# Three buffers instead of four for rounded weight tiles, and one expert chunk loaded earlier

## The reference

```python
h = rms_norm(x, g_mix)
proj = h @ w_in + b_in                       # q, k, v, r, gates, ...
mixed = sigmoid(gate_a) * (o_a @ w_gla_out) + sigmoid(gate_b) * (o_b @ w_swa_out)
x = x + mixed @ w_out
logits = rms_norm(x, g_ffn) @ w_router + b_router        # top 4 of 32
u = xb @ w_e1[e] + b_e1[e]                   # for each expert: 1024 x 2048
act = clamped_swiglu(u)
y = act @ w_e2[e] + b_e2[e]                  # 1024 x 1024
out = rms_norm(x + combine(y), g_final)
```

## Time and profile before

| what | value |
|---|---|
| median of 3 executions | 1175.7 us (1175.5 to 1176.05) |
| the profiled execution | 1175.9 us, its span 1174.1 us |
| PE busy | 1125.6 us (96%) |
| DVE, ACT, POOL busy | 434.7, 257.0, 38.0 us |
| read from HBM | 446.12 MB |
| mean granted clock of TensorE | 0.998 |

### The profile page before, as it was taken

One profiled execution on the slowest core, in us unless ns is written; L12 is line 12 of the kernel. 1 busy time (PEld: TensorE's weight loads), 2 busy tenths in 40 slices (PEclk: granted clock), 3 DMA queues, 4 the chain that ended last, 5 costly groups with the idle time before them and its releaser, 6 DMA issues.

```text
span 1174.1 us, 17495 instructions
## 1 busy us (share of the span) xinstructions
PE 1125.6 (96%) x7259; PEld 538.5 (46%) x7259; DVE 434.7 (37%) x832; ACT 257.0 (22%) x445; POOL 38.0 (3%) x30
## 2 busy tenths in 40 slices
PE   7999999999999999999999999999999999999997
PEld 6987889983333333333333333333333333333332
DVE  6889956954322222222222222222222222222223
ACT  5467745332111111111111111111111111111112
POOL 1001600011000000000000000000000000000000
PEclk9999999999999999999999999999999999999999
DMA  8645337789999999999999999999999999999995
GB/s 298 231 155 206 144 136 268 283 354 420 427 428 427 435 430 429 430 444 431 438 433 429 436 429 435 438 433 433 431 435 431 424 431 434 432 432 430 431 424 236
DMA packets 23202, 447.66 MB, mean 381 GB/s; under 512 B 2736, under 2 KB 3120, under 8 KB 5344
## 3 DMA queue, kind: packets, MB, share of 16 engines
q1 hardware_dynamic: 22736, 446.76, 90.2%
q10 hardware_dynamic: 432, 0.42, 0.1%
HBM read 446.12 MB, written 1.05 MB: 381 GB/s over the span
## 4 chain that ended last, share of the span: by engine, by line
PE 58%; DMA 29%; DVE 9%; ACT 2%; issue 1%; POOL 1%; DVEq 0%; SPq 0%; another core or an unknown queue 0%; ACTq 0%
PE PS L943 35%; DMA EXT<-wexp 20%; PE PS L667 11%; DMA ring<-wexp 8%; PE PS L936 3%; PE PS L928 3%; PE PS L959 2%; DVE slot_R L1361 1%; PE PS L716 1%; DVE ROW L1817 1%; DVE ROW L1820 1%; DVE BRW L1813 1%; DVE ROW L1814 1%; DVE SM L1549 1%; DVE ring L1544 1%
## 5 line engine op out<-in xcount | busy, mean ns | idle before, releaser
L943 PE MATMUL PS<-ring,MX 128*64 128x512 f32 x1536 | 349.6, 597 | 11.3 <-DMA ring<-wexp 10.7
L943 PEld LDWEIGHTS PS<-ring,MX 128*64 128x64 f32 x1536 | 103.6, 136 | 221.6 <-issue 199.5
L1308 ACT ACTIVATE TAB<-BRW 128x256 f32<-128x256 f32 x64 | 26.7, 417 | 587.0 <-DVE BRW L1813 587.0
L943 PE MATMUL PS<-EXT,MX 128*64 128x512 f32 x512 | 116.9, 598 | 7.9 <-DMA EXT<-wexp 7.8
L943 PE MATMUL PS<-ring,TAB 128*64 128x512 f32 x512 | 120.0, 600 | 4.1 <-DMA ring<-wexp 4.1
L943 PE MATMUL PS<-EXT,TAB 128*64 128x512 f32 x512 | 119.5, 598 | 0.5 <-DMA EXT<-wexp 0.5
L1813 DVE TENSOR_SCALAR BRW<-PS 128x256 f32<-128x256 f32 x64 | 27.2, 425 | 241.2 <-PE PS L943 241.2
L667 PE MATMUL PS<-slot_R 128*128 128x256 f32 (+2 forms) x288 | 90.2, 313 | 0.0
L1361 DVE TENSOR_TENSOR slot_R<-ring,slot_R 128x2048 fp32r<-128x2048 f32 (+1 forms) x37 | 83.1, 2262 | 13.4 <-ACT slot_R L1100 13.1
L1100 ACT ACTIVATE slot_R<-ring 128x2048 fp32r<-128x2048 f32 (+1 forms) x38 | 70.8, 1869 | 45.2 <-PE PS L667 24.1
L936 PE MATMUL PS<-MX,BRW 64*128 64x512 f32 x264 | 74.2, 640 | 0.8 <-DVE MX L1832 0.8
(11 more groups left out here) (263 smaller groups left out, 1083.4 us busy)
## 6 DMA issues: line engine op xcount, KB each, us to landing
ring<-wexp SPq DMA_DIRECT2D x23, 4096.0 KB, 41.4
ring<-wexp SPq DMA_DIRECT2D x22, 2048.0 KB, 13.0
EXT<-wexp SPq DMA_DIRECT2D x10, 4096.0 KB, 40.1
ring<-wblk SPq DMA_DIRECT2D x36, 1024.0 KB, 4.9
EXT<-wexp SPq DMA_DIRECT2D x13, 2048.0 KB, 13.8
ring<-wexp SPq DMA_DIRECT2D x8, 1024.0 KB, 10.4
EXT<-wexp SPq DMA_DIRECT2D x6, 1024.0 KB, 47.6
BRW<-brow SPq DMA_DIRECT2D x7, 256.0 KB, 5.1
```

Of the source, the lines that this page charges most:

```text
L943: last = mm(PS[g * SLOTS:(g + 1) * SLOTS, b, :], lhsT, rhs[:, g * 512:(g + 1) * 512], start=start, stop=stop)
L1308: fn(SGM[h], GLU, ACT.Sigmoid, scale=ALPHA).then_inc(sgm_ready, 1)
```

## The change

- `h_slot`: up to unit 28 (`GIVEN`) the rounded tiles go round four places as before, from unit 29 on round three of them. `split(u)` waits for the unit that held its place, `held_before`; for units 32 to 37 this is `u - 3` instead of `u - 4`.
- The place that is given up is next to slot 0, and the two slots take chunk 4. `C_FIRST` (chunk 4) leaves the list `MIDDLE` and is issued right after the weight load of unit 34 (`FIRST_AT`), that is, once unit 29 has been multiplied. `last_of` gives the unit after which a slot is free.
- ACT rounds the last two parts of the mixed tensor before `split(36)`, not after it.
- DVE's `rest(36)` moves from before the reads of block 16 to after them.

```diff
-W_SLOTS = [1, 2, 4, 6, 8]
-H_SLOTS = [3, 5, 7, 9]
+W_SLOTS = [2, 3, 4, 6, 8]
+H_SLOTS = [1, 5, 7, 9]
...
-MIDDLE.insert(1, C_SQ)
+C_FIRST = MIDDLE.pop(0)
+MIDDLE.insert(0, C_SQ)
...
+GIVEN = 2 * BLOCKS.index("glao1")
+FIRST_AT = GIVEN + 6
...
+        def h_slot(u):
+
+            if u <= GIVEN:
+                return (u - GIVEN) % len(H_SLOTS)
+            return 1 + (u - GIVEN - 1) % (len(H_SLOTS) - 1)
+
+        def held_before(slot_fn, u):
+
+            return max((n for n in range(u) if slot_fn(n) == slot_fn(u)), default=None)
+
+        def last_of(slot_fn, q):
+
+            return max(n for n in range(NU) if slot_fn(n) == q)
...
-            return slot(H_SLOTS[(u - (NU - len(H_SLOTS))) % len(H_SLOTS)], rounded)[:, 0:unit_width(u)]
+            return slot(H_SLOTS[h_slot(u)], rounded)[:, 0:unit_width(u)]
...
-                elif c in MIDDLE:
+                elif c in MIDDLE or c == C_FIRST:
                     for n in (2 * s, 2 * s + 1):
                         if n in W_SLOTS:
-                            multiplied(sp, NU - len(W_SLOTS) + W_SLOTS.index(n))
+                            multiplied(sp, last_of(w_slot, W_SLOTS.index(n)))
                         elif n in H_SLOTS:
-                            multiplied(sp, NU - len(H_SLOTS) + H_SLOTS.index(n))
+                            multiplied(sp, last_of(h_slot, H_SLOTS.index(n)))
...
                 if u == FREE_AT:
                     first_chunk(C_FREE)
+                if u == FIRST_AT:
+                    first_chunk(C_FIRST)
...
                 landed(act, u)
-                if u >= len(H_SLOTS):
-                    multiplied(act, u - len(H_SLOTS))
+                held = held_before(h_slot, u)
+                if held is not None:
+                    multiplied(act, held)
                 fn(h_unit(u, True), w_unit(u), ACT.Copy).then_inc(hi_ready, 1)
...
             split(NU - 3)
-            split(NU - 2)
             for c in range(2, 4):
                 act.wait_ge(mix_ready, c + 1)
                 fn(MIX2[0][:, 2 * c:2 * c + 2, :].rearrange("p k t -> p (k t)"), MIX[c], ACT.Copy).then_inc(mix_hi, 1)
+            split(NU - 2)
             split(NU - 1)
...
                     rest(35)
-                    rest(36)
+            rest(36)
             rest(37)
```

## The result

The changed kernel takes 1178.34 us (median of 14 executions, 1176.32 to 1180.23) against 1176.14 us for the kernel before beside it (14 executions, 1175.38 to 1177.57). The ratio is 1.0018, 95% interval 1.0011 to 1.0025: 2.2 us slower, 0.18%. The forecast was 1175.5 us with a range up to 1177.6 us; the time lies 0.7 us above the range. The profiled execution took 1177.18 us (span 1175.3 us).

The account below looks back on a forecast made before the run. The prediction took DMA throughput as the bound. PE's 2.3 us wait minus 2.0 to 3.1 us of queue removed gave +0.3 to -0.8 us, middle -0.2 us: 1175.5 us against the median 1175.7 us, range 1173.2 to 1177.6 us.

Parts of the forecast that it names:

- The sum: Chunk 2's time moves by PE's 2.3 us wait minus 2.0 to 3.1 us of queue; middle -0.2 us.
- a rival at 0.10: Clock halves in PE's new wait; a half unit, 2.9 us of work, runs slow: 1178.3 us in the middle; chance 0.10.
- the stall: PE's wait in block 15's second half near 220.7 us for a bank whose read stands behind rest(32): 2.3 us, once.
- The row that I had: Behind the last matmul the granted clock is 1.00 for 2.0 us, then 0.68 over 0.6 us, then 0.50.
- the queue removed: Transfers queued in front of chunk 2, issued at 263.83 us, that loading chunk 4 early takes away: 2.0 to 3.1 us.
- by bytes: Queue in front of chunk 2 reckoned from bytes moved between 241.09 and 272.10 us: 2.0 us.
- by landings: Queue in front of chunk 2 from times to landing, 10.3 us against chunk 4's 7.2 us: 3.1 us.
- The thin covers downstream: Later bank reads and roundings stay ahead of PE despite DVE's delay; thinnest at block 16, 1.3 us.
- The collision of chunk 4 with unit 35's load: Unit 35's load, at worst behind chunk 4, lands by about 231 us, hidden with 4 us to spare.
- The end is set by DMA: DMA throughput sets the end: share 1.00 at 432 GB/s from 300 to 1155 us; PE has 23.1 us of slack.
- Parts 3 and 4: The moved roundings on ACT and the moved rest(36) on DVE cost nothing.
- The first rival: PE's new wait is absent or covered, so 2.0 to 3.1 us are gained: 1172.6 to 1173.7 us; chance 0.12.

Follow-up runs that it names:

- buffers_only: Changed kernel with chunk 4 issued where it was before, after unit 33 and ahead of chunk 10: 1179.02 us, ratio 1.0021.
- fill_stall: Changed kernel with 18 matmuls of 128 x 256, whose result nobody reads, added on PE inside its wait for the bank: 1176.67 us, ratio 1.0010.
- half_stall: Changed kernel with DVE's rest(32) cut in two, the second half behind the first two reads of block 14: 1175.32 us, ratio 0.9993.
- no_stall: Changed kernel with DVE's rest(32) moved behind block 14's reads and biases1(1): 1173.97 us, ratio 0.9985.
- before_again: The kernel before, run again with no edit: 1175.72 us, ratio 0.9999.
- before_pause: The kernel before with 12 matmuls of 128 x 256, whose result nobody reads, added in unit 34: 1175.97 us, ratio 0.9996.
- after_again: The changed kernel, run again with no edit: 1178.07 us, ratio 1.0018.

## Why the prediction was wrong

**What failed.** The sum has no term for the clock: it takes 1.00 throughout, and leaves the fall to a rival at 0.10. That step failed. The fall is the commonest case, in 11 of the 14 executions, and it puts 1.4 to 1.5 us on top of the stall. I held against it that PE is busy without a gap on both sides. The runs showed that this does not save it: the clock fell 1.2 us after PE had resumed in one profile and at once in another (buffers_only), and stayed low for about 3.4 us of full work. The row that I had, 2.0 us at full clock behind the last matmul and less after it, spoke for far more than 0.10. The rule that the prediction cited for this rival (the Trainium skill, TensorE: Matmul & The Clock Gate, Part 1) agrees in kind with the profile in which the clock is 0.52. How short a wait is enough, and what the fall costs, only the runs show. The rival's price was off too: 2.9 us for a half unit of work at half clock, where 1.4 to 1.5 us was measured. That its 1178.3 us is near the measured 1178.34 us is luck: the price of the fall is 1.4 us too high, and the rest of the sum 1.2 us too low.

**The queue in the sum was mis-sized as well.** With the stall at full clock I forecast 1175.5 us; fill_stall, which is that case, takes 1176.67 us. The stall was right (2.37 us against 2.3 us). For the queue removed I took the middle between 2.0 us by bytes and 3.1 us by landings, about 2.5 us. The early chunk was worth 2.0 us against the kernel before, and 1.6 us against the kernel that differs in it alone. So the figure by bytes was the nearer one, and averaging the landings in made 0.5 to 0.9 us of the 1.2 us. The rest is not settled. It lies within the spread of single executions: five of fill_stall's 11 take 1177.98 us or more at an unchanged clock, and the other six 1176.09 to 1176.67 us. The first profile of the changed kernel shows the same spread. PE's delay is that of fill_stall's profile to 0.01 us, but from the weight load of unit 33 to the issue of the last long link it has 860.52 us against 859.82 us in fill_stall (859.27 us in the kernel before), so 0.7 us lie between two executions that have the stall and the early chunk in common and no fall of the clock.

How the queue runs dry can be seen between 264 and 268 us, before and after:

```profile
264.00:268.00 4.00, 3.40 (x27) 1.42 (x25) 2.66 (x8) 2.56 (x6) 2.73 (x3) 1.00 1.06 438
```

```profile
264.00:268.00 4.00, 4.00 (x28) 2.73 (x26) 1.29 (x3) 2.56 (x6) 1.66 (x2) 1.00 0.79 295
```

A share of 1.06 becomes 0.79. This is the cap on the gain and not one more cost: fill_stall and half_stall, profiled at 1176.09 and 1175.03 us, have the same dip (0.79 and 0.80, both 279 GB/s). It also fits the bytes. A lone chunk has moved 6.3 us after its issue, and 4.85 us of that is transfer, so its bytes begin some 1.4 us after the issue; chunk 2's then begin at about 267.6 us, while those of chunk 7, which landed at 267.6 us, had ended about 0.9 us (7.2 - 6.3) before. That is an estimate of 0.9 us without transfers, and a share of 0.79 over 4 us lacks 0.84 us.

**What held.**

- The place and length of the stall: 2.3 us forecast, 2.37 us by the issues, one wait, released by L1684's read; `rest(32)` at 220.05 us, the read at 222.26 us, PE at 223.00 us, against 220.07, 222.3 and 223.05 us forecast.
- The thin covers downstream all held, at block 16 and before unit 35.
- The collision of chunk 4 with unit 35's load cost nothing, although in the first profile chunk 4 landed only 12.1 us after its issue, at 230.5 us, not 227.6 us.
- The end is set by DMA: the share is 1.00 at 432 GB/s from 300 to 1155 us before and after, and PE's waits for weights are 22.0 us instead of 23.1 us.
- Parts 3 and 4 and the third buffer itself cost nothing (1175.61 us with `rest(32)` moved as well).
- The first rival, no stall, gave 1172.6 to 1173.7 us; measured 1173.97 us, 0.3 us above its upper end.

In the medians the early chunk is -2.0 us (no_stall), the stall at full clock +2.7 us (fill_stall over no_stall), and the fall of the clock +1.4 us. That they make +2.1 us is no check, since each is the difference to the one before. The check is PE's own delay, read from the issues: 2.37 us for the stall, 0.3 us less than in the medians, and 1.47 us for the fall.

**Open.** Why some executions, three of 11 in before_again, are nearly 2 us longer at an unchanged clock. One of them was profiled (before_pause, 1177.84 us), and nearly all its extra time is there long before the expert part: a weight load that is issued at 23.76 us in the kernel before (23.42 us in before_again) is issued at 25.48 us, and the weight load of unit 33 at 213.96 us instead of 212.29 us (211.87 us). The first eight matmuls of L716, at 12.20 us, take 3.75 us there instead of 2.06 us, with the granted clock at 1.00; why is not known. Open too are why the fall is rarer in buffers_only (three of 11) than in the changed kernel (19 of 24), and how much queue there is for half a chunk.

## To carry to other kernels

When a tile buffer is given up, look for the consumer that stands behind the newly late step in an in-order engine's list: here one `rest` ahead of a bank's read cost twice what the freed space brought, and moving it behind the read turned a loss of 2.2 us into a gain of 2.0 us. Where transfers are the bound, first measure the queue at the narrowest issue: here it capped what an earlier load gained (2.0 of 4.85 us), and once it was spent, a pause of PE that had been free began to count. A wait of PE of some 2 us in the midst of dense work should be priced with the clock's fall, and repeated executions looked at, since one profile can miss it.

## What the runs showed of the hardware

After a wait of 2.1 us between full stretches of matmuls the granted clock fell to 1.2 GHz in 19 of 24 executions of the changed kernel, judged by a mean clock of 0.997 or less, and in at least three of 11 of buffers_only. In the two profiles that show it the fall came 1.2 us after the matmuls had resumed (after_again) and as they resumed (buffers_only), and lasted about 3.4 us. With a wait of 1.1 us (half_stall) the clock stayed up in the profile, and no mean clock of the 11 executions was under 0.998. Eighteen useless matmuls in the gap kept it up and saved 1.4 us. On the chunks that PE times one by one, the DMA engines' share dipped to 0.79 over 4 us, although the next transfer (chunk 2, at 266.19 us) was issued before the one in front of it had landed (chunk 7, at 267.6 us): being issued ahead of a landing by 1.4 us was not enough to keep the engines busy.
